# Gate and up projections of 18 of 22 feature tiles by seven half-size products, in stages of 4, 6, 6 and 6 tiles

## The reference

```python
def swiglu(h, w_gate, w_up, w_down):
    return (jax.nn.silu(h @ w_gate) * (h @ w_up)) @ w_down

for l in range(DEPTH):
    mx = (silu(c) @ w_mod[l] + b_mod[l]).reshape(B, 9, 1, D)      # mc the same from c_ctx
    x  = x  + 0.5 * mx[:, 2] * swiglu(modulate(rms_norm(x),  mx[:, 0], mx[:, 1]), w_ffn_gate[l, 0], ...)
    xc = xc + 0.5 * mc[:, 2] * swiglu(modulate(rms_norm(xc), mc[:, 0], mc[:, 1]), w_ffn_gate[l, 0], ...)
    yx, yc = token_mixing(...)                                    # attention, window attention, pooling
    x = x + mx[:, 5] * yx
    x = x + 0.5 * mx[:, 8] * swiglu(...)                          # context too, unless the layer is the last
```

## Time and profile before

| | |
|---|---|
| Median of 3 runs | 2888.7 us (2886.15 to 2889.39) |
| Profiled execution: span of its trace | 2885.3 us |
| Busy: TensorE, VectorE, ScalarE | 2805.7, 1481.8, 947.1 us (97, 51, 33%) |
| Matmuls | 16327 |
| DMA | 262.99 MB, mean 91 GB/s |

### The profile page before, as it was taken

How to read it: one execution, slowest core, us unless ns; L and a number is a source line. 1 busy time by engine, 2 the same in 40 slices (tenths; PEclk the granted TensorE clock), 3 DMA queues, 4 the chain that set the end, 5 groups by cost and what they waited for, 6 DMA issues and landing times.

```text
span 2885.3 us, 42478 instructions
## 1 busy us (share of the span) xinstructions
PE 2805.7 (97%) x16327; PEld 2647.6 (92%) x16327; DVE 1481.8 (51%) x2293; ACT 947.1 (33%) x1526; POOL 262.8 (9%) x279
## 2 busy tenths in 40 slices
PE   7999999999988899999999999999999998999999
PEld 5999999989977889999999999999998987888887
DVE  6554355455477665533553555245346587633332
ACT  4221122233388641211222422112233388532231
POOL 1000000031234210000000100000003234000000
PEclk9999999999999999999999999999999999999999
DMA  6433243223100224322442244233223201233333
GB/s 227 135 119 99 84 134 122 83 63 78 32 14 14 77 88 124 120 84 89 135 127 65 81 124 127 62 117 118 74 62 88 57 14 50 78 95 107 90 100 90
DMA packets 361093, 262.99 MB, mean 91 GB/s; under 512 B 11087, under 2 KB 339189, under 8 KB 359953
## 3 DMA queue, kind: packets, MB, share of 16 engines
q1 hardware_dynamic: 359440, 256.86, 29.6%
q10 hardware_dynamic: 896, 4.46, 0.4%
q0 software_dynamic: 640, 0.09, 0.0%
HBM read 255.08 MB, written 2.10 MB: 89 GB/s over the span
## 4 chain that ended last, share of the span: by engine, by line
PE 90%; ACT 4%; DVE 3%; issue 1%; POOL 0%; DMA 0%; SPq 0%; POOLq 0%; ACTq 0%; DVEq 0%
PE pair L426 24%; PE pair L427 24%; PE pair L434 24%; PE pair L1310 2%; PE pmid L2113 2%; PE pair L1312 2%; PE pair L1311 2%; PE pair L681 2%; PE pair L682 2%; PE pair L683 2%; ACT pt_hi L2167 1%; PE psum L2139 1%; PE pair L2094 1%; ACT prob L2182 1%; PE psum L2141 1%
## 5 line engine op out<-in xcount | busy, mean ns | idle before, releaser
L426 PE MATMUL pair<-h_lo,w_hi 128*128 128x384 f32 (+1 forms) x2656 | 907.4, 343 | 0.7 <-ACT sg L1101 0.4
L427 PE MATMUL pair<-h_hi,w_hi 128*128 128x384 f32 (+1 forms) x2656 | 906.3, 343 | 0.0
L426 PEld LDWEIGHTS pair<-h_lo,w_hi 128*128 128x128 f32 x2656 | 499.2, 188 | 23.0 <-issue 0.6
L427 PEld LDWEIGHTS pair<-h_hi,w_hi 128*128 128x128 f32 x2656 | 499.4, 188 | 21.5
L402 DVE TENSOR_TENSOR w_lo<-w_raw,w_hi 128x1024 fp32r<-128x1024 f32 (+1 forms) x262 | 349.1, 1333 | 323.6 <-ACT w_hi L395 320.4
L434 PE MATMUL pair<-h_hi,w_lo 128*128 128x384 f32 (+1 forms) x2656 | 513.7, 343 | 0.0
L434 PEld LDWEIGHTS pair<-h_hi,w_lo 128*128 128x128 f32 x2656 | 463.4, 188 | 20.6
L395 ACT ACTIVATE w_hi<-w_raw 128x1024 fp32r<-128x1024 f32 (+1 forms) x262 | 296.0, 1130 | 540.2 <-PE pair L434 508.9
L426 PE MATMUL pair<-s_lo,w_hi 128*128 128x384 f32 (+1 forms) x1100 | 377.7, 343 | 0.0
L427 PE MATMUL pair<-s_hi,w_hi 128*128 128x384 f32 (+1 forms) x1100 | 377.2, 343 | 0.0
L948 DVE SCALAR_TENSOR_TENSOR pmid<-mod_raw,cs_rows 128x1024 f32<-128x1024 f32 x256 | 315.1, 1231 | 76.5 <-DMA mod_raw<-in_w_mod_rows 59.6
(11 more groups left out here) (310 smaller groups left out, 3600.9 us busy)
## 6 DMA issues: line engine op xcount, KB each, us to landing
mod_raw<-in_w_mod_rows SPq DMA_DIRECT2D x64, 1024.0 KB, 4.9
w_raw<-in_w_ffn_gate SPq DMA_DIRECT2D x88, 512.0 KB, 3.8
w_raw<-in_w_ffn_up SPq DMA_DIRECT2D x88, 512.0 KB, 3.8
w_raw<-in_w_ffn_down SPq DMA_DIRECT2D x64, 704.0 KB, 4.7
w_raw<-in_w_in SPq DMA_DIRECT2D x32, 512.0 KB, 4.0
w_raw<-in_w_out SPq DMA_DIRECT2D x12, 512.0 KB, 4.2
w_raw<-in_w_q_up SPq DMA_DIRECT2D x8, 576.0 KB, 4.1
mod_first<-in_w_mod ACTq DMA_DIRECT2D x4, 1024.0 KB, 9.2
```

The source lines that it names most:

```text
L426: eng.matmul(dst, wh, rl, start=k == 0, stop=False)
L427: eng.matmul(dst, wh, rh, start=False, stop=False)
```

## The change

In ff0, ff1 and ff2 the feature tiles come in four stages: 4 tiles as before, then three stages of 6 tiles each. The down product follows each stage (over 4 or 6 chunks), so each output tile is formed and added to xT four times. ff3 has stages of 8, 8 and 6 tiles in the old way.

In a stage of 6 the tiles go in three pairs. The gate (and then the up) product of two feature tiles is a 2 by 2 by 2 block product: two halves of the width (4 chunks each), two features, two halves of the tokens (384 each). Eight half-size products would do it; it is done by seven, over sums and differences of weight blocks and of token blocks. Each product is 4 chunks by three matmuls of 384 columns (L1138 to L1140) into one PSUM bank. Products that several results need are kept in one bank: ScalarE copies the bank to SBUF (L1339, `pair_copy`), TensorE goes on adding the next product into the same bank, and VectorE adds the copy to what the bank holds then (L1346, `pair_comb`). The sums of weight blocks are made on VectorE (`pair_sum`, four of 128 by 512 for each group of seven), the seven high parts on ScalarE (L1294), the seven low parts on VectorE (L1306). The sums of token blocks are made once in a block, during stage 0 (`token_sums`, eight instructions of 128 by 1536, then `token_hi` and `token_lo`, four each).

Weight blocks have seven slots (high and low); the raw gate or up weights of a pair come in one load of 1 MB into one of two buffers, which the raw down tiles share. The row dots are placed by MOD_PLAN: in stage 0, in the pairs, and within the down products. The loops of the FFN blocks are unrolled.

```diff
-FF_TILES = 2 * (2 * HALF + KD)
+FF_PLAN = [[(4, 0), (0, 3), (0, 3), (0, 3)]] * 3 + [[(8, 0), (8, 0), (6, 0)]]
...
+    counts = [
+        [("up", 0, i) for i in range(4)] + [("pair", 1, p) for p in range(3)] + [("down", 1, i) for i in range(4)] +
+        [("pair", 2, p) for p in range(3)] + [("down", 2, i) for i in range(4)] + [("pair", 3, p) for p in range(3)] +
+        [("down", 3, i) for i in range(3)],
...
+        [("up", 0, i) for i in range(1, 5)],
+    ]
...
+            if j in (2, 5):
+                eng.wait_ge(g_copied, 3 * g + (1 if j == 2 else 2))
+            if j == 4:
+                eng.wait_ge(g_copied, 3 * g + 3)
+            if j == 6:
+                eng.wait_ge(g_comb, 3 * g + 2)
+            (mh, ml), dst, first = MOVING[j], product_bank(up, j), j in (0, 1, 3)
+            for k in range(KD // 2):
+                wh, wl = p_hi[n][:, k * P:(k + 1) * P], p_lo[n][:, k * P:(k + 1) * P]
+                eng.matmul(dst, wh, ml[:, k, :], start=first and k == 0, stop=False, skip_group_check=True)
+                eng.matmul(dst, wh, mh[:, k, :], start=False, stop=False, skip_group_check=True)
+                last = eng.matmul(dst, wl, mh[:, k, :], start=False, stop=k == KD // 2 - 1, skip_group_check=True)
+            last.then_inc(g_prod, 1)
...
+                for i in range(KD // 2):
+                    planned_load(eng, inst, ("down", s, i))
+                    if i == 0 and inst < 3 and 0 < s and not last_stage:
+                        pair_load(eng, inst, s + 1, 0, 0)
+                    if i < KD // 2 - 1:
+                        for d in range(2 * i + 2, 2 * i + 4):
+                            ff_down_load(eng, inst, s, d)
...
+                    pair_comb(eng, inst, s, p, up, 3)
+                    planned_dot(eng, inst, at, up, 0)
+                    pair_comb(eng, inst, s, p, up, 4)
...
+                    if d < KD - 2:
+                        for j in range(2):
+                            planned_dot(eng, inst, ("down", s, d // 2), d % 2, j)
...
+                        else:
+                            for j in (5, 6):
+                                pair_lo(eng, inst, s + 1, 0, 0, j)
+                            for j in range(4):
+                                planned_dot(eng, inst, ("down", s, KD // 2 - 1), j // 2, j % 2)
```

More of the change, by code:

```diff
@@ L127 @@
         FF_O0.append(_o)
-        WIDTHS += ([KD * P] * (2 * HALF) + [HALF * P] * KD) * 2
-        _o += FF_TILES
+        FF_STAGES.append([])
+        _f = 0
+        for _n, _pairs in FF_PLAN[2 * _l + _fi]:
+            _chunks = _n + 2 * _pairs
+            FF_STAGES[-1].append(dict(t0=len(WIDTHS), o0=_o, n=_n, pairs=_pairs, chunks=_chunks, f0=_f, g0=_groups))
+            WIDTHS += [KD * P] * (2 * _n) + [_chunks * P] * KD
+            _o += 2 * _n + KD
+            _f += _chunks
+            _groups += 2 * _pairs
         if _fi == 0:
@@ new lines, in group, with raw_of, w_block, chunked @@
+        def group(inst, s, p, up):
+            return FF_STAGES[inst][s]["g0"] + 2 * p + up
+        def raw_of(s, up):
+            return gate_raw(s) if not up else 1 - gate_raw(s)
+        def w_block(x, feature, k):
+            return x[:, 4 * k:4 * k + 4, feature * P:(feature + 1) * P]
+        def chunked(x):
+            return x.rearrange("p (k m) -> p k m", m=P)
+        def h_block(x, k, half):
+            return x[:, 4 * k:4 * k + 4, half * (TOK // 2):(half + 1) * (TOK // 2)]
+        MOVING = [(h_block(h_hi, 0, 0), h_block(h_lo, 0, 0)), (t_hi[0], t_lo[0]), (t_hi[1], t_lo[1]),
+                  (h_block(h_hi, 1, 0), h_block(h_lo, 1, 0)), (h_block(h_hi, 0, 1), h_block(h_lo, 0, 1)),
+                  (h_block(h_hi, 1, 1), h_block(h_lo, 1, 1)), (t_hi[2], t_lo[2])]
@@ L1000, in ff_pe @@
                 if crossing:
-                    tail_pe(eng, X_NORM[NEXT_BLOCK[inst]], ff_tail(inst), HALF, s_moving)
+                    tail_pe(eng, X_NORM[NEXT_BLOCK[inst]], ff_tail(inst), st["chunks"], s_moving,
+                            [down_lhs(inst, s, KD - 2 + j) for j in range(2)])
                 if final:
@@ new lines, in pair_into, with pair_copy @@
+        def pair_into(inst, s, p, up, feature, half):
+            cols = slice(half * (TOK // 2), (half + 1) * (TOK // 2))
+            return ff_u(inst, 2 * p + feature)[:, cols] if up else sg[:, feature, cols]
+        PLACE_OF = {0: (0, 0), 1: (1, 1), 2: (0, 1), 3: (0, 0), 4: (1, 1), 5: (0, 1)}
+        def pair_copy(eng, inst, s, p, up, j):
+            g = group(inst, s, p, up)
+            eng.wait_ge(g_prod, 7 * g + j + 1)
+            if not up and j == 0 and g >= 2:
+                eng.wait_ge(g_mul, 4 * (g // 2))
+            eng.activation(pair_into(inst, s, p, up, *PLACE_OF[j]), product_bank(up, j), ACT.Copy).then_inc(g_copied, 1)
@@ L1242, in mod_pairs_through @@
         def mod_pairs_through(inst):
-            lasts = [last_pair(i, half) for i in range(inst + 1) for half in range(2)] + \
-                [v for i in range(inst + 1) for v in FF_EXTRA[i]]
-            return max(v for v in lasts if v is not None) + 1
+            return PAIR_0 + sum(len(plan) for plan in MOD_PLAN[:inst + 1])
         def mod_pairs_before(l):
```

671 lines of the change are left out of this document (499 added, 172 removed), and 4 rows, old and new, of the table FF_SEGS.

## The result

| | before | changed |
|---|---|---|
| Median of 18 runs | 2888.8 us (2886.2 to 2892.1) | 2895.2 us (2890.1 to 2902.5) |
| Ratio | | 1.0024, 95% interval 1.0017 to 1.0031 |
| Span of the profiled execution | 2885.3 us | 2895.5 us |

What follows compares the result with a forecast made beforehand. TensorE's matmuls were taken to bound the kernel: 112.3 us saved against 119 of new waits, +6.5, taken as +10 with handoffs, plus 15 for the clock: 2913 us, 0.9% slower; 8-in-10 range 2864 to 2944.

Steps and rivals of the forecast that it cites:

- the clock's step: After the new TensorE waits, 9 of 24 were taken to bring a fall to half clock, 1.7 us each: +15 us.
- What is removed: FFN gate and up products: 84 matmuls for 96 per pair group, 648 fewer, 112.3 us saved; unrolling gains nothing.
- Term 1: End of stage 0, three blocks: TensorE waits for s_lo and the first residual behind VectorE's queue, 19.5 us.
- Term 2: Down tiles of stages 1 and 2: loads stand behind mod_raw's, which waits for four dots; 35 us.
- Term 3: From last down tile to next pairs: waits for a bank's copy, 22 us, and ahead of product 6, 7 us.
- Term 4: Inside the pairs: VectorE's work barely fits beside TensorE's; 0.33 us at each of 15 gate groups, 5 us.
- Term 5: Ways out of the FFN blocks: 15 us after ff0 (dots, norm chain), 2 each for the other two.
- Term 6: ff3's first stage: tiles 1 to 4 with dots take 13.9 us each instead of 10.88, 10 us.
- The 4 us allowed for handoffs: Allowance for handoffs between engines, which the terms had priced at 0 to 0.2 us.
- The rival with every fall counted: The clock falls after every long TensorE wait, costing 41 us: 2940 us, chance 0.18.
- The faster rival: At the down tiles, loads don't hold them back, SyncE's turn at or under 12.5 us: 2853 us, chance 0.14.

Runs made afterwards that it cites:

- e4: Changed kernel with the last two token sums and token low parts moved from stage 0's end to behind the residuals of down tiles 0 to 4: 2874.5 us.
- e2: Changed kernel with the down tiles' loads ahead of mod_raw's load in SyncE's stream, except in a stage's first turn: 2847.3 us.
- e3: Changed kernel with the dots within the down products cut to 8 elements and their loads left out (27 of 64): 2826.0 us.
- e5: Changed kernel with ff3's four loads of row dots moved to ff1 (three) and ff2 (one): 2887.8 us.
- e6: Changed kernel with e2 and e4 together, ff3's row dots moved, and no dots behind a stage's last down tile in ff1 and ff2: 2805.9 us.
- e1: Changed kernel with extra matmuls into an unused bank filling TensorE's waits at down tiles 2, 4, 6 and product 4: 2893.1 us.

## Why the prediction was wrong

The forecast had 2910 us for the profiled execution, 15 above what was measured. About 6 of the 15 are the clock's step, which added falls to waits as if neither touched the other; about 9 are waits worked out too long. Further falls at ff0's end and in ff3, which weren't priced, would move this split towards the waits. The rest of the miss is the distance between profiled executions and medians told above.

- **What is removed** (648 matmuls, 112.3 us): right. The pairs of stage 1 take 88.1 us for 504 matmuls of 0.1733, and unrolling shows nothing in ff3's later stages or the mixers.
- **Term 1**: the waits were 14.7 + 2.5 = 17.2 for 19.5; with the clock 24.0. e4 shows the cause of the larger one.
- **Term 2**: 35 foretold, 37.4, in which the falls at tiles 4 and 6 are. The turn is 15.4 for 15.7, and e2 takes the term away by the queue alone.
- **Term 3**: 29 foretold, 22.8 with the clock inside. The working of product 4 held to 0.2 us where it was followed row by row. The waits ahead of product 6 are 3.3 us, four times; 7 in five were foretold.
- **Term 4**: 0.7 for a stage's two later gate groups, the 0.33 each that was put down. In stages 2 and 3 it is inside row 3 of the table.
- **Term 5**: 19 foretold, 24.4, above all in ff1 and ff2, where shorter cover cost 4.4 and 3.1 for 2 each. In ff0, its larger part, e3 takes 13.3 of 16.9 away.
- **Term 6**: 10 foretold, 10.1; e5.
- **The waits are a little too long all through.** At a stage end tile 4 began 1.8 to 2.1 us late for the 2.4 worked out, tile 6 another 2.8 to 3.1 for 3.2 to 3.5, product 4 3.35 for 3.6. The 4 us allowed for handoffs were not there. The prediction says that its waits' ends were rounded down; they were not. That is some 9 us, and it hides in the sum behind what the clock cost.
- **The clock**: the step whose mechanism failed. It took 9 falls after the new waits and put each with 1.7 us on top of the waits: +15. There were 15 new falls and two longer ones in the second mixer; the mean clock lost 49 us of full-speed time against 12 before, 38 more. Yet what could be priced of them added about 9 us, not 15. Terms 2 and 3 are set by an engine other than TensorE, and ahead of such a deadline a slow TensorE only waits less: from tile 6 to product 4 it is 24.1 to 24.2 us with a fall or without. The waits and the falls were added as if they stood side by side. Where no deadline follows a fall did cost: behind stage 0 about 2 us each, and 2 in the pairs of ff0's stage 3.
- **The rival with every fall counted** (2940) has the same fault, larger. The faster rival, that the loads don't hold the tiles back, is refuted by the turn of 15.4 us; for the cure it put 60 us, and e2 gained 48.

Left open: the changed kernel's 18 runs spread over 12 us, before's over 6, and go with the clock: the two fastest show 0.986, the three slowest 0.981 and 0.982. The 0.004 to 0.005 is 12 to 14 us of full-speed time, so falls that come in one run and not in the next seem to cost nearly all they take. The kept traces have such falls: behind stage 0 a fall lasts 3.4 us in one block and 6.8 in another, and a fall of 6.8 behind product 4 comes at one stage end in six. Whether these make the spread isn't shown; the changed kernel's profile is of one run. Nor was it tried to price the seven products with no dots in the FFN blocks at all.

## What to carry to other kernels

Find for each wait what sets its end. A loss that comes before a wait set by another engine is taken out of that wait and is not added to it; count it only where the bound engine has no deadline behind. And when loads of two users share an in-order queue, ask which waits for what: here a prefetch that waited for four dots held up weights that had no need to wait, 48 us, for one exchange of two lines. Work that saves matmuls on the bound engine has to come with a plan for the engine that takes its place at the ends of stages, where e6 found 89 of the 123 us that had come back as waits.

## What the runs showed of the hardware

- A fall came even in dense stretches: 2.73 us of waiting, then 3.4 us at 0.50, with matmuls without a gap on both sides. The length of the wait alone did not decide it: in ff0's stage 2 of the changed kernel a fall came 1 us after a wait of 1.94 us, and in ff2 of e4 waits of 2.48 and 3.06 us passed in two rows at 1.00. With the waits filled (e1), those stretches stayed at 1.00.
- A 1 MB load issued directly behind mod_raw's 1 MB took 7.7 us at the median (14 gate loads) and 7.6 (6 up loads); the other gate and up loads took 5.4 and 5.3. The page's medians mix the two cases:

```profile
p_raw<-in_w_ffn_gate SPq DMA_DIRECT2D x27, 1024.0 KB, 7.4
p_raw<-in_w_ffn_up SPq DMA_DIRECT2D x27, 1024.0 KB, 5.4
```
